# Sixteen experts on TensorE: the transposes of the expert tokens, done by halves of the array's rows

## What is computed

```python
def run_expert(args):
    ix, gt, wg, wu, wd = args
    xe = h[bidx, ix]                              # 128 tokens x 1024
    he = jax.nn.silu(xe @ wg) * (xe @ wu)         # 128 x 2048
    return (he @ wd) * gt[..., None]              # 128 x 1024
ys = lax.map(run_expert, (idx_e, gates_e, w_gate, w_up, w_down))
return jnp.zeros_like(h).at[jnp.arange(b)[None, :, None], idx_e].add(ys)
```

## Time and profile before

| | us |
|---|---|
| median of the 3 runs | 2182.87 |
| the profiled execution | 2185.03 |
| its span, first to last instruction | 2183.1 |
| TensorE busy in the span | 2069.7 (95%) |
| VectorE busy | 1612.3 (74%) |
| ScalarE busy | 1245.2 (57%) |
| experts: first product to last | 1080 to 2172 |

### The profile page before, as it was taken

The page is one execution under the profiler, slowest core; times in us unless marked ns, Lnnn a source line. Parts: engine busy times, 40 slices in busy tenths (PEclk is TensorE's granted clock), DMA queues, the critical chain, the costliest instruction groups (busy, mean ns, idle before and its releaser), DMA issues.

```text
span 2183.1 us, 25951 instructions
## 1 busy us (share of the span) xinstructions
PE 2069.7 (95%) x9987; PEld 1687.2 (77%) x9987; DVE 1612.3 (74%) x1530; ACT 1245.2 (57%) x1135; POOL 150.3 (7%) x105
## 2 busy tenths in 40 slices
PE   6999989999999999997399999999999999999997
PEld 4778777788878777785288888888888888888886
DVE  6777657588865422444688989989899898988985
ACT  4422146277764311333277777777777777777774
POOL 4000000100000000000300000000000000000000
PEclk8999999999999999998599999999999999999999
DMA  8565120211113211136299999999999999999994
GB/s 283 161 185 167 39 58 2 63 44 44 44 44 97 83 44 44 64 122 240 102 354 380 386 382 392 386 385 375 386 393 386 386 383 380 391 383 382 386 380 155
DMA packets 245113, 510.87 MB, mean 234 GB/s; under 512 B 7692, under 2 KB 64312, under 8 KB 245048
## 3 DMA queue, kind: packets, MB, share of 16 engines
q1 hardware_dynamic: 236496, 484.71, 60.6%
q0 software_dynamic: 5952, 18.88, 3.4%
q10 hardware_dynamic: 2600, 6.38, 1.3%
HBM read 486.88 MB, written 16.78 MB: 231 GB/s over the span
## 4 chain that ended last, share of the span: by engine, by line
PE 50%; DMA 0%; DVE 0%; POOL 0%; issue 0%; ACT 0%; DVEq 0%; POOLq 0%
PE ps_gu L2156 32%; PE ps_down L2156 16%; PE ps_turn L2151 2%; DMA moe_x<-h_rows,slot_token 0%; POOL out_x L2136 0%; DVE moe_x_lo L2086 0%; ACT moe_x_hi L2052 0%; DVE moe_y L2108 0%; DVEq L1986 0%; POOLq L1646 0%
## 5 line engine op out<-in xcount | busy, mean ns | idle before, releaser
L2080 DVE TENSOR_TENSOR h_lo<-tiles,h_hi 128x2048 fp32r<-128x2048 f32 x252 | 565.9, 2287 | 73.9 <-ACT h_hi L2047 72.2
L2047 ACT ACTIVATE h_hi<-tiles 128x2048 fp32r<-128x2048 f32 x252 | 468.8, 1911 | 79.1 <-PE ps_down L2156 46.8
L2080 DVE TENSOR_TENSOR third_split<-tiles,third_split 128x2048 fp32r<-128x2048 f32 x128 | 287.4, 2286 | 41.4 <-ACT third_split L2047 40.4
L2047 ACT ACTIVATE third_split<-tiles 128x2048 fp32r<-128x2048 f32 x128 | 238.1, 1911 | 39.0 <-PE ps_down L2156 25.7
L2156 PE MATMUL ps_gu<-h_hi,moe_x_hi 128*128 128x512 f32 x640 | 251.9, 394 | 2.5 <-DVE moe_x_lo L2086 2.5
L2156 PE MATMUL ps_gu<-h_hi,moe_x_lo 128*128 128x512 f32 x640 | 250.3, 391 | 0.0
L2156 PE MATMUL ps_gu<-h_lo,moe_x_hi 128*128 128x512 f32 x640 | 249.9, 391 | 0.0
L2156 PE MATMUL ps_gu<-third_split,moe_x_hi 128*128 128x512 f32 x768 | 239.6, 393 | 0.0
L298 PE MATMUL ps_projected<-h_hi,hi_ring 128*128 128x512 f32 x496 | 194.2, 391 | 4.0 <-DVE lo_ring L285 2.0
L298 PE MATMUL ps_projected<-h_hi,lo_ring 128*128 128x512 f32 x496 | 193.1, 389 | 0.0
L298 PE MATMUL ps_projected<-h_lo,hi_ring 128*128 128x512 f32 x496 | 193.0, 389 | 0.0
(11 more groups left out here) (340 smaller groups left out, 3736.5 us busy)
## 6 DMA issues: line engine op xcount, KB each, us to landing
tiles<-in_w_gate SPq DMA_DIRECT2D x64, 2048.0 KB, 10.0
tiles<-in_w_up SPq DMA_DIRECT2D x64, 2048.0 KB, 10.6
tiles<-in_w_down SPq DMA_DIRECT2D x64, 2048.0 KB, 10.9
tiles<-in_w_ada SPq DMA_DIRECT2D x24, 1024.0 KB, 8.3
tiles<-in_w_in SPq DMA_DIRECT2D x17, 1024.0 KB, 5.5
tiles<-in_w_in SPq DMA_DIRECT2D x16, 512.0 KB, 5.4
tiles<-in_w_lru_branch SPq DMA_DIRECT2D x8, 1024.0 KB, 5.1
v<-v ACTq DMA_DIRECT2D x48, 128.0 KB, 2.4
```

Source lines behind the costliest of these rows:

```text
L2047: nc.scalar.activation(half(w_hi(t), i), half(raw_tile(g, t), i), ACT.Copy).then_inc(hi_ready, 1)
L2080: nc.vector.tensor_tensor(half(w_lo(t), i), half(raw_tile(g, t), i), half(w_hi(t), i).bitcast(F32), ALU.subtract).then_inc(lo_ready, 1)
```

## The change

A turn no longer takes 128 tokens at a time. Each transpose takes a chunk of 128 columns of one half of the tokens: 64 partitions, so one half of the array's rows, with 64 columns of the identity to move. The two halves follow each other (q = 0, 1), and half q writes PSUM bank q. So a turn of hidden values has 8 transposes in place of 4, a turn of x 16 in place of 8. The copies that read the result read the two banks in turns of 64 elements. The waits of a turn move ahead of the last chunk of the tile before it: 3 matmuls earlier at a gate or up tile, 6 at a down tile.

```diff
         def turn_view(what):
             if what == "x":
-                return flat_turn, x_hi[:, :, :].rearrange("p c n -> p (c n)"), x_lo[:, :, :].rearrange("p c n -> p (c n)")
-            return (ps_turn[:, what % 2, :], h_hi[:, what, :, :].rearrange("p c n -> p (c n)"),
-                    h_lo[:, what, :, :].rearrange("p c n -> p (c n)"))
+                turned_in, hi, lo = ps_turn[:, :, :], x_hi[:, :, :], x_lo[:, :, :]
+            else:
+                turned_in = ps_turn[:, :, UNIT * (what % 2):UNIT * (what % 2 + 1)]
+                hi, lo = h_hi[:, what, :, :], h_lo[:, what, :, :]
+            halves = lambda ap: ap.rearrange("p c (q n) -> p c q n", n=HD)
+            return turned_in.rearrange("p q (c n) -> p c q n", n=HD), halves(hi), halves(lo)
...
                 dst = turn_view(what)[0]
                 for c in range(n):
-                    ins = nc.tensor.transpose(dst[:, c * P:(c + 1) * P], src[:, c * P:(c + 1) * P], ident)
+                    for q in range(2):
+                        rows = slice(HD * q, HD * (q + 1))
+                        ins = nc.tensor.transpose(dst[:, c, q, :], src[rows, c * P:(c + 1) * P], ident[rows, rows])
                 ins.then_inc(turned, 1)
+            def before_turn(e, t, last):
+                if t not in TURNS or (last and TURNS[t] == "x"):
+                    return
+                what = TURNS[t]
+                if what == "x":
+                    pe.wait_ge(gathered, e * 16 + 32)
+                    pe.wait_ge(turn_lo, turns_before(e, "x"))
+                else:
+                    pe.wait_ge(hidden_ready, e * 4 + what + 1)
+                    if what == 3:
+                        pe.wait_ge(turn_lo, (e * 5 + 4) if last else turns_before(e, 3))
...
                             for c in range(2 * i, 2 * i + 2):
+                                if c == 3:
+                                    before_turn(e, t, last)
...
                             for c in range(4 * i, 4 * i + 4):
+                                if c == KC - 1:
+                                    before_turn(e, t, last)
...
                     ins.then_inc(tile_done, 1)
-                    if t in TURNS:
-                        what = TURNS[t]
-                        if what == "x":
-                            if last:
-                                continue
-                            pe.wait_ge(gathered, e * 16 + 32)
-                            pe.wait_ge(turn_lo, turns_before(e, "x"))
-                        else:
-                            pe.wait_ge(hidden_ready, e * 4 + what + 1)
-                            if what == 3:
-                                pe.wait_ge(turn_lo, (e * 5 + 4) if last else turns_before(e, 3))
-                        turn(what)
+                    if t in TURNS and not (last and TURNS[t] == "x"):
+                        turn(TURNS[t])
```

## The result

The changed kernel takes 2193.36 us, the median of 5 runs (2192.27 to 2194.25), beside 2183.8 us for the kernel before in the same session (2182.64 to 2184.97). The ratio is 1.0042, with a 95% interval of 1.0031 to 1.0052: slower by 9.6 us. Forecast were +9.0 us and 2191.9 us.

A forecast was written before the change was run, and what follows sets the result against it. TensorE alone was taken to bound the kernel. Hidden-values turns 64 x 0.16 = 10.2, x turns 15 x -0.05 = -0.8, first x turn -0.4: together +9.0 us, 2191.9 us, range 2179.5 to 2198 us.

The forecast's parts named there:

- the first turn of x: Turn on an idle TensorE, before and behind: its transposes shrink from 0.87 to 0.52 us, giving -0.4 us.
- the unit of hidden values: Start of last product before a hidden-values turn to start of second behind: 0.90 us becomes 1.04.
- the detour: Leaving the full array and returning each turn: 0.34 us at the router, from emptying each way and unhidden loads.
- Rival D: At a turn's joints, no emptying either way: -18.6 us, 2164.3 us; 0.11 together with what lies down to it.
- none of the joints of the old turns costs anything: Around the old turns on TensorE: a turn is nothing but its transposes, 0.109 us each; joints and waits cost nothing.
- the 0.02 us for the products behind: Products following a new turn: 0.04 us too much behind the router, 0.02 behind the old turn, so 0.02 added.
- The round: Two half-transposes together, 128 columns of all tokens: 0.053 to 0.06 us, taken as 0.057, replacing one transpose of 0.109.
- x's unit: Start of last product before a turn of x to start of second behind: 1.34 us becomes 1.27.
- Rival B: Within a turn, half-transposes get no cheaper, loads sharing a path or instructions too slow: +28.8 us, 2211.6 us; chance 0.11.
- The moved waits: Waits moved ahead of a tile's last products by 0.68 or 1.36 us: all met in time, costed at nothing.
- the copies: ScalarE and VectorE reading two banks by turns of 64: bounded by 0.5 us for x, taken as nothing.

The follow-up runs named there:

- the useless pair: Kernel before plus one unused pair of half-array transposes behind tiles 0 and 1 of every expert: 2199.10 us, ratio 1.0072.
- the eight pairs: Kernel before plus eight unused pairs of half-array transposes behind tiles 0 and 1 of every expert: 2212.23 us, ratio 1.0127.

## Why the prediction was right

**What bounds it.** TensorE alone did before, and does now; the expert's length moved by what its turns did, 68.08 to 68.70 us, where 68.67 was forecast. The chain's times are rounded; with the 68.09 of the earlier trace rows the growth is 0.61. Sixteen times that, less the 0.4 that the first turn of x gave back (the first product stands at 1080.03 us instead of 1080.40), is 9.4; the span grew by 2192.2 - 2183.1 = 9.1 us. Each term of the sum held by itself, so the agreement is not luck in the main. Only in the unit of hidden values do two small errors cancel: the detour was put at 0.36 us and is 0.35, four rounds were put at 0.23 and take 0.24.

**The detour, read from the router.** This was the largest term and it held: 0.34 us by the router, 0.36 once its small loads and its stagger are exchanged for those of the transposes, and 0.35 by the useless pair, although the router leaves the whole array for quarters of its columns and the change for halves of its rows. The unit of hidden values is 1.04 us as worked out. Rival D has fallen with it. One reading ahead of it was wrong: that none of the joints of the old turns costs anything. Inside the unit nothing shows, but the tile behind is 0.03 to 0.04 us longer than an undisturbed one. It did not hurt the sum, since units were compared with units and the 0.02 us for the products behind was a difference too.

**The round** was mis-sized by a little: 0.062 us against 0.057, the middle between moving columns and load. Neither moving columns nor instructions set it, and the reading of the load from the earlier trace rows (0.06) would have given it. Over eight rounds that makes x's unit 1.29 us instead of 1.27, so the turn of x gains 0.05 and not 0.07 by its unit, and with the 0.02 that trail behind it 0.03 and not 0.05. The last round of a turn holds only its moving columns, 0.053 us, so with four rounds the error is 0.01 and hidden values stay at 0.16 within the rounding of the rows. With -0.03 for x the sum becomes 10.2 - 0.5 - 0.4 = +9.3; the span shows 9.1 and the medians 9.6, both inside the interval. The Trainium skill (TensorE: Matmul & The Clock Gate, LDWEIGHTS) puts 128 columns at 0.107 us; for these fp32 transposes the eight pairs measure 0.063. The product behind a turn, whose load is seen in full, comes nearer to the page: the next begins 0.33 us after it instead of 0.227, so 0.10 us for 128 columns. Rival B, which that rule would have brought about for the transposes, did not come.

**The moved waits** cost and gave nothing, as costed. So did **the copies**: the low part of x is written in as long as before, though it reads two banks by turns of 64.

```profile
1616.87 1.22 DVE L2089 TENSOR_TENSOR moe_x_lo<-ps_turn,moe_x_hi 128x1024 fp32r<-128x1024 f32 x1
```

The Trainium skill (TensorEngine Tiling (Array Packing), Overview and Key Properties) has both sides of this case, up to twice the speed for small dimensions, and an emptied array with each change of mode. The first holds inside the detour (0.062 us instead of 0.109), the second is what decides, and it is the second that needs a number: 0.35 us, 0.39 with what trails.

## What to carry to other kernels

Count chunks before tiling the array. Going to part of it and back cost 0.39 us here and saved 0.047 us per 128x128 transpose; a whole-array turn has a joint of 0.04 itself, so (0.39 - 0.04) / 0.047, between seven and eight transposes, must stand together before it pays: x with eight gained 0.03, hidden values with four lost 0.16 each time. The price was read in advance from another place of the same kernel where TensorE leaves the whole array; the unit for that runs from the last full matmul to the second one behind.

## What had not been expected of the hardware

TensorE takes transposes of one half of the rows up beside those of the other although they stand several instructions later: four upper then four lower ran in 1.06 us, as good as in pairs (1.04), while eight then eight came only part of the way (1.60 against 1.29). The loads of that run, above, say the same: alone, they follow each other every 0.06 us, as the first five of x do, while at the start of the turn of hidden values they come two by two. Two into one half could not, so there is one for each half, though four transposes of the upper half were written ahead of the lower's first. The Trainium skill (TensorE: Matmul & The Clock Gate, Part 3) says that matmuls start strictly in program order and only loads are pulled ahead; with the fifth matmul behind the fourth, and steps of 0.06 us within a half, the eight could not begin within 0.25 us, so the trace does not agree. How far ahead TensorE looks was not tried, why the turn of x begins with five loads alone stays open, and the trace does not name the half of a transpose, so this rests on the times alone.

A single whole transpose between two tiles costs 0.17 us, not its 0.109; one of a turn of four or eight costs 0.109 and its share of 0.04.
